# Mixer output of a two-block transformer: gate, grouped norm and output projection in one stage, by token halves

## The chip, the cores and the metric

The kernel runs on one core of a Trainium2 chip. The metric is the time of one execution in microseconds (us), the median of the timed runs. The core has a matrix engine (TensorE, PE in the rows; its weight loads are PEld), a vector engine (VectorE, DVE), an activation engine (ScalarE, ACT), a general engine (GpSimd, POOL) and a sync engine (SyncE, SP) that here only issues transfers. Each engine runs its own instruction list in order; they meet at semaphores.

## The reference

The whole model is two blocks, a mixer with a mixture of experts and then attention with a feed-forward network, for 1024 tokens of width 1024. The change touches the end of the first block's mixer only. There, `y` is the output of the state-space scan (768 channels in 4 groups), `xh` its input, `z` the gate, `y_pool` the 256 channels of a second mixer, `g1` a vector from the conditioning:

```
y = ssd_scan(xh, dt, a, bm, cm) + xh * d_skip
y = y.reshape(b, s, 768) * silu(z)
y = rms_norm(y.reshape(b, s, G, 768 // G)).reshape(b, s, 768)
y_ssd = y * norm_w
mix = concatenate([y_pool, y_ssd], axis=-1) @ w_out
x = x + g1[:, None, :] * mix
h = modulate(x, sh2, sc2)      # its router logits are h @ [w_group, w_router]
```

## The kernel before

Everything is kept transposed: the 128 partitions hold channels, and the free axis the 1024 tokens, so a tensor of 768 channels is 6 tiles of 128x1024 (`SSD_T` = 6) and one of 1024 channels 8 (`KT` = 8). Work is written as stages, one after another. A stage opens its own buffers and semaphores and gives each engine a list; the next stage begins on an engine when all engines have left the one before. Inside a stage `st.dve(ins, "name")` counts an instruction up on its engine's semaphore, and `st.wait(e, st.dve, "name")` waits for it. `settle()` waits for the engine's own last instruction.

`gate_norm` (L963) is the stage after the scan. VectorE makes the gated `y` in place in `xbc[:, 6+j]` with two instructions a tile (L1021, L1023); ScalarE squares it into `zs`, which lies in the buffer of `x` (L1001). TensorE sums the squares over the channels of each group: `member` is a 128x4 matrix of zeros and ones for each tile, so a product with it gives 4 rows of 1024 sums, accumulated over the 6 tiles (L986). VectorE and ScalarE turn these 4x1024 numbers into reciprocal root mean squares (L1025, L1027, L1003). TensorE spreads the 4 rows back over 128 partitions, one product with `member_t` a tile, alternating between two PSUM buffers (L993). Then for each tile VectorE multiplies `y`, the spread factor and the norm weight into `tmp` (L1032), ScalarE rounds it to the high part `xh_mix` (L1006) and GpSimd subtracts to get the low part `xl_mix` (L1013); `tmp` has two buffers, so VectorE waits for GpSimd two tiles back.

`mixer_out` (L1037) is the next stage: 8 output tiles of the projection. Every product of the big projections is made of three, high times high, low times high and high times low (`Gemm.mult`, L239 in the rows): 8 input tiles x 3 x 2 token halves of 512 = 48 matmuls an output tile. The weights of an output tile are 128x1024; they are loaded (L215 for the first two, L200 for the rest), and split into high and low parts by VectorE for the first two (`Gemm.first`, L221 and L223) and by GpSimd for the rest (`Gemm.split`, L207 and L209). VectorE then clears `acc`, scales the router's weights `w_route`, builds `wide` (a matrix of shifts for the router), and for each output tile adds the product to `x` (L1108) and the squares to `acc` (L1111). ScalarE loads `x` back from memory (L1086, 4 MB), as its buffer held `zs`, and later squares and stores `x`.

The next stages (`route`, `experts`) read `x`, `acc` and the logits; they issue their first transfers when `mixer_out` is left.

## Time and profile before

| | |
|---|---|
| median of 3 runs | 2595.18 us (2594.09 to 2597.12) |
| the profiled execution | 2599.4 us, of which the span of the profile is 2597.6 us |
| mean granted TensorE clock | 0.902 of 2.4 GHz |
| TensorE busy (matmul) | 2251.2 us, 87% |
| VectorE busy | 1306.2 us, 50% |
| ScalarE busy | 801.6 us, 31% |
| GpSimd busy | 607.2 us, 23% |

The profile is one execution; times in its rows count from the start of the span. A busy share is a mean over the whole program, and says little on one stage: the stages here take from about 505 to 674 us.

### The profile page before, as it was taken

To read this page: it belongs to the slowest core of one execution; us is meant where nothing else is said; L and a number is where in the kernel's file an instruction comes from. 1 tells how busy PE (TensorE), PEld (TensorE's weight loads), DVE (VectorE), ACT (ScalarE), POOL (GpSimd) and SP (SyncE) were. 2 spreads that over 40 slices of the span, in tenths; PEclk is the share of its full clock that TensorE was granted. 3 is DMA by queue.
4 is the path that set the end of the run, shared out by engine and by line. 5 is a ranking of instruction groups with operands and counts; after the bars stand their busy time and mean duration, and the time that the engine had idled before them with its cause. 6 is when DMAs were issued, how large, how long until landed. Compare 5 with 4: busy or idle time off the path is not lost. (4 is left out here: it accounts for less than half of the span.)

```text
span 2597.6 us, 44356 instructions
## 1 busy us (share of the span) xinstructions
PE 2251.2 (87%) x15928; PEld 1689.1 (65%) x15928; DVE 1306.2 (50%) x1615; ACT 801.6 (31%) x1108; POOL 607.2 (23%) x444
## 2 busy tenths in 40 slices
PE   2699978869754897898977897998999999999998
PEld 1588867638622454454536786776888888888887
DVE  7676165732443686786865536773433213321344
ACT  3211122310233676786863103551210000000013
POOL 0133313222000000000003462222333333333344
PEclk6799977769766998998986998999999999999999
DMA  6333210022699998899954120001111111111113
GB/s 250 144 121 121 91 66 0 1 105 75 254 380 410 363 356 293 320 352 339 337 194 171 57 90 5 0 0 57 48 49 48 49 49 48 48 49 49 48 50 120
DMA packets 103785, 364.19 MB, mean 140 GB/s; under 512 B 7968, under 2 KB 18848, under 8 KB 103344
## 3 DMA queue, kind: packets, MB, share of 16 engines
q1 hardware_dynamic: 85248, 320.43, 34.1%
q10 hardware_dynamic: 13008, 23.07, 2.3%
q0 software_dynamic: 5472, 19.93, 2.2%
q8 instruction: 36, 0.59, 0.1%
q14 instruction: 21, 0.17, 0.0%
HBM read 331.94 MB, written 31.46 MB: 140 GB/s over the span
## 5 line engine op out<-in xcount | busy, mean ns | idle before, releaser
L1488 PE MATMUL moe_hu<-x_res,moe_xt 128*32 128x256 f32 x5120 | 336.4, 406 | 83.2 <-DVE moe_xt L1404 55.7
L1382 DVE COPY x_res<-moew_raw 128x2048 f32 x243 | 270.2, 1135 | 188.0 <-DMA moew_raw<-in_w 110.4
L1488 PEld LDWEIGHTS moe_hu<-x_res,moe_xt 128*32 128x32 f32 x5120 | 163.2, 116 | 213.0 <-issue 90.4
L239 PE MATMUL ff_acc<-ff_yh,ff_w_hi 128*128 128x512 f32 x704 | 274.4, 390 | 0.0
L239 PE MATMUL ff_acc<-ff_yl,ff_w_hi 128*128 128x512 f32 x704 | 273.9, 389 | 0.0
L239 PE MATMUL ff_acc<-ff_yh,ff_w_lo 128*128 128x512 f32 x704 | 273.9, 389 | 0.0
L1382 ACT ACTIVATE x_res<-moew_raw 128x2048 f32 (+1 forms) x121 | 197.2, 1630 | 108.9 <-DMA moew_raw<-in_w 77.7
L207 POOL CAST ff_w_hi<-ff_w_raw 128x1024 fp32r<-128x1024 f32 (+1 forms) x82 | 81.9, 998 | 545.5 <-PE ff_acc L239 545.5
L239 PE MATMUL ff_acc<-xh,ff_w_hi 128*128 128x512 f32 x480 | 188.2, 392 | 7.8 <-DVE ff_w_lo L223 7.1
L239 PE MATMUL in_acc<-xh_mix,in_w_hi 128*128 128x512 f32 x368 | 144.4, 392 | 55.5 <-DVE in_w_lo L223 55.5
L209 POOL TENSOR_TENSOR ff_w_lo<-ff_w_raw,ff_w_hi 128x1024 fp32r<-128x1024 f32 (+1 forms) x82 | 188.7, 2301 | 6.6
L239 PE MATMUL ff_acc<-xh,ff_w_lo 128*128 128x512 f32 x480 | 187.3, 390 | 0.0
L239 PE MATMUL ff_acc<-xl,ff_w_hi 128*128 128x512 f32 x480 | 187.2, 390 | 0.0
L1393 ACT ACTIVATE moe_wdown<-moew_raw 128x2048 f32 x80 | 153.2, 1915 | 25.9 <-PE moe_y L1499 22.0
L1499 PE MATMUL moe_y<-moe_wdown,moe_at 128*32 128x256 f32 x2560 | 157.5, 387 | 2.4 <-ACT moe_at L1533 2.4
L239 PEld LDWEIGHTS ff_acc<-ff_yh,ff_w_hi 128*128 128x128 f32 x704 | 132.1, 188 | 28.0 <-DVE ff_yl L2307 0.5
L239 PEld LDWEIGHTS ff_acc<-ff_yh,ff_w_lo 128*128 128x128 f32 x704 | 132.2, 188 | 27.6
L239 PEld LDWEIGHTS ff_acc<-ff_yl,ff_w_hi 128*128 128x128 f32 x704 | 132.2, 188 | 27.5 <-issue 0.2
L1445 POOL COPY moew_idx<-rows 128x1 int32 (+1 forms) x21 | 11.2, 534 | 578.4 <-PE moe_xturn L1471 578.4
L239 PE MATMUL in_acc<-xl_mix,in_w_hi 128*128 128x512 f32 x368 | 144.1, 392 | 0.0
L239 PE MATMUL in_acc<-xh_mix,in_w_lo 128*128 128x512 f32 x368 | 144.1, 392 | 0.0
L2258 ACT ACTIVATE ff_gs<-ff_gs 128x1024 f32<-128x1024 f32 x22 | 23.3, 1061 | 379.7 <-DVE ff_gs L2318 379.7
(354 smaller groups left out, 3942.3 us busy)
## 6 DMA issues: line engine op xcount, KB each, us to landing
moew_raw<-in_w SPq DMA_DIRECT2D x192, 1024.0 KB, 18.9
ff_w_raw<-in_w_up SPq DMA_DIRECT2D x44, 512.0 KB, 3.3
mid_w_raw<-in_w_qkv SPq DMA_DIRECT2D x24, 512.0 KB, 3.3
in_w_raw<-in_w_in SPq DMA_DIRECT2D x23, 512.0 KB, 3.3
x_res<-in_w_ada SPq DMA_DIRECT2D x20, 512.0 KB, 5.2
y_scratch<-acc_sq ACTq DMA_DIRECT2D x80, 128.0 KB
prep_wa<-in_w_ada SPq DMA_DIRECT2D x18, 512.0 KB, 6.1
ff_w_raw<-in_w_down SPq DMA_DIRECT2D x16, 512.0 KB, 3.3
```

Of the source, the lines that this page charges most:

```text
L207: pool.tensor_copy(hi, raw).then_inc(self.s_hi, 1)
L209: pool.tensor_tensor(lo, raw, hi.bitcast(F32), ALU.subtract).then_inc(self.s_split, 1)
L239: m = pe.matmul(o, w[:, b, k * P:(k + 1) * P], x[:, k, h:h + HALF], start=(k == 0 and t == 0), stop=(k == kt - 1 and t == 2))
L1382: m = e.activation(to, src, ACT.Copy) if k == "act" else e.tensor_copy(to, src)
L1393: m = e.activation(to, src, ACT.Copy) if k == "act" else e.tensor_copy(to, src)
L1445: e.tensor_copy(idx[:, :], self.rows[:, g:g + 1] if isinstance(g, int) else self.rows[:, bass.ds(g, 1)]).then_inc(s_idx, 1)
L1488: m = e.matmul(hu[u % 2][rows(j), 0:2 * FW].rearrange("p (a f) -> p a f", a=2), xt[:, t, rows(u)], w[:, :, FW * j:FW * (j + 1)], start=(t ...
L1499: m = e.matmul(yp[u % 2][rows(j), 0:YW], at[:, t % KC, rows(t // KC)], wdown[:, t, YW * j:YW * (j + 1)], start=(t == 0), stop=(t == FF // ...
L2258: st.act(e.activation(gs[:, :], gs[:, :], ACT.Silu), f"silu{n}")
```

## The change

`gate_norm` is gone as a stage; its work stands at the head of `mixer_out`'s lists.

- Group sums: `member` is padded to 32 columns (4 of them used), and each tile's product is four, one for each quarter of the tokens (256), on the column quarters (0, 32q) of the array. The sums stand on 4 x 32 partitions x 256 tokens in place of 4 x 1024, and so do the two VectorE instructions and the root after them.
- Spreading: in 12 steps (token half h, tile j), each of two products of 256 tokens on the row quarters (64h+32q, 0), which write two PSUM banks. The second `total` buffer is the projection's `acc1`.
- Norm, high and low part: 12 steps of 512 tokens; the product is written in place into `y`; VectorE now makes the low part too, one step behind (`low`).
- The first output tile goes by token halves (`first_product`), each input tile waiting for its own low part.
- The weights and `wr` are requested at the stage's start, behind `member` and `member_t` (now 96 KB and 384 KB); semaphores are cleared after that. VectorE splits the first two weight tiles between the reciprocal and the norm steps. ScalarE loads the table of the root ahead of its wait, and requests `x` right behind the root.
- Clearing `acc`, scaling `w_route` and building `wide` move from VectorE to GpSimd, ahead of its splits. `sq` takes two dead tiles of `xbc`.

The diff, with the removed stage left out (it is printed above):

```
                 self.s_spill = ctx.enter_context(nc.semaphore("x_spilled"))
                 self.mixer_out()
             with self.stage("moew") as self.weights:
@@ -960,100 +959,45 @@
...
-            with st.block() as blk:
...
-        self.keep.close()
...
     def mixer_out(self):
 
         x, acc, ins = self.x, self.acc_sq, self.ins
+        xbc, zs, Q = self.xbc, self.zs, T // 4
         R = EG + NE
         with self.stage("mixout") as st:
             g = Gemm(st)
-            sq, wide, wr = st.sb("sq", [P, 2, T]), st.sb("wide", [P, KT, P]), st.sb("wr", [P, KT, R])
+            wide, wr = st.sb("wide", [P, KT, P]), st.sb("wr", [P, KT, R])
+            sq = xbc[:, 0:2, :]
+            member, member_t = st.sb("member", [P, SSD_T, 32]), st.sb("member_t", [P, SSD_T, P])
+            rstd = st.sb("rstd", [P, Q])
             logits, shifted = st.ps("logits", [P, HALF]), st.ps("shifted", [P, HALF])
-            s_x, s_wr = st.sem("x"), st.sem("wr")
+            group_sum = logits[:, 0:Q]
+            total = [a.rearrange("p (b x) -> p b x", b=2)[:, :, 0:Q] for a in (st.ps("total", [P, T])[:, :], g.acc[1][:, :])]
+            s_x, s_wr, s_member = st.sem("x"), st.sem("wr"), st.sem("member")
+            halves = [slice(h * HALF, (h + 1) * HALF) for h in range(2)]
+            steps = [(h, j) for h in range(2) for j in range(SSD_T)]
+            y = lambda h, j: xbc[:, SSD_T + j, halves[h]]
             with st.block() as blk:
                 @blk.sync
                 def _(e):
+                    e.dma_start(member[:, :, :], ins["member"]).then_inc(s_member, 16)
+                    e.dma_start(member_t[:, :, :], ins["member_t"]).then_inc(s_member, 16)
                     g.first(sp=e, srcs=[ins["w_out"][b] for b in range(2)])
                     e.dma_start(wr[:, :, :], ins["w_route"]).then_inc(s_wr, 16)
+                    self.clear_sems(e)
                     with e.Fori(0, KT // 2 - 1) as i:
                         for b in range(2):
                             g.load(e, i, 2, b, ins["w_out"][2 * i + (2 + b)])
...
                 @blk.gpsimd
                 def _(e):
+                    st.pool.start(e)
+                    st.pool(e.memset(acc[:, :], 0.0))
+                    e.wait_ge(s_wr, 16)
+                    scale, shift = self.mod[:, 32:40], self.mod[:, 24:32]
+                    st.pool(e.tensor_tensor(self.w_route[:, :, :], wr[:, :, :], scale.unsqueeze(2).to_broadcast([P, KT, R]), ALU.mult))
+                    for k in range(KT):
+                        st.pool(e.tensor_scalar(wide[:, k, :], self.const("ones"), shift[:, k:k + 1], None, ALU.mult), "wide")
                     g.after_first(e)
                     with e.Fori(0, KT // 2 - 1) as i:
                         for b in range(2):
...
                 def _(e):
                     st.pe.start(e)
                     e.sem_inc(g.s_mult, 2)
+                    e.wait_ge(s_member, 32)
+                    for j in range(SSD_T):
+                        st.wait(e, st.act, f"gate_sq{j}")
+                        for q in range(4):
+                            m = e.matmul(group_sum[32 * q:32 * q + 32, :], member[:, j, :], zs[:, j, q * Q:(q + 1) * Q],
+                                         start=(j == 0), stop=(j == SSD_T - 1), tile_position=(0, 32 * q))
+                    st.pe(m, "group_sum")
+                    st.wait(e, st.act, "rstd")
+                    for n, (h, j) in enumerate(steps):
+                        if n >= 2:
+                            st.wait(e, st.dve, "normed%d%d" % steps[n - 2])
+                        for q in range(2):
+                            rows = slice(64 * h + 32 * q, 64 * h + 32 * q + 32)
+                            m = e.matmul(total[n % 2][:, q, :], member_t[rows, j, :], rstd[rows, :],
+                                         start=True, stop=True, tile_position=(64 * h + 32 * q, 0))
+                        st.pe(m, f"spread{h}{j}")
+
+                    def first_product():
+                        e.wait_ge(g.s_split, 3)
+                        e.wait_ge(g.s_emptied, 1)
+                        for h in range(2):
+                            for k in range(KT):
+                                if k >= POOL_T:
+                                    st.wait(e, st.dve, f"lo{h}{k - POOL_T}")
+                                for t, (w, xs) in enumerate(((g.hi, self.xh), (g.hi, self.xl), (g.lo, self.xh))):
+                                    m = e.matmul(g.acc[0][:, halves[h]], w[:, 0, k * P:(k + 1) * P], xs[:, k, halves[h]],
+                                                 start=(k == 0 and t == 0), stop=(k == KT - 1 and t == 2))
+                        m.then_inc(g.s_mult, 1)
 
...
                     for k in range(KT):
-                        g.mult(e, k // 2, 0, k % 2, self.xh, self.xl)
+                        if k:
+                            g.mult(e, k // 2, 0, k % 2, self.xh, self.xl)
+                        else:
+                            first_product()
                         if k == 0:
-                            st.wait(e, st.dve, "wide")
+                            st.wait(e, st.pool, "wide")
                             for j in range(KT):
                                 m = e.matmul(shifted[:, 0:R], wide[:, j, :], wr[:, j, :], start=(j == 0), stop=(j == KT - 1))
...
                 @blk.scalar
                 def _(e):
                     st.act.start(e)
+                    for j in range(SSD_T):
+                        st.wait(e, st.dve, f"gated{j}")
+                        st.act(e.activation(zs[:, j, :], xbc[:, SSD_T + j, :], ACT.Square), f"gate_sq{j}")
+                    e.preload_act_table(ACT.Sqrt)
+                    st.wait(e, st.dve, "inv")
+                    st.act(e.activation(rstd[:, :], rstd[:, :], ACT.Sqrt), "rstd")
                     e.dma_start(x[:, :, :], self.xt_dram).then_inc(s_x, 16)
+                    for h, j in steps:
+                        st.wait(e, st.dve, f"normed{h}{j}")
+                        st.act(e.activation(self.xh[:, POOL_T + j, halves[h]], y(h, j), ACT.Copy), f"hi{h}{j}")
                     for k in range(KT):
                         g.emptied(e, k // 2, 0, k % 2)
                         if k >= 2:
...
                 def _(e):
                     st.dve.start(e)
                     e.sem_inc(g.s_emptied, 2)
+                    for j in range(SSD_T):
+                        st.dve(e.scalar_tensor_tensor(xbc[:, SSD_T + j, :], xbc[:, j, :], self.col("d_skip", j), xbc[:, SSD_T + j, :], ALU.mult, ALU.add))
+                        st.dve.settle()
+                        st.dve(e.tensor_tensor(xbc[:, SSD_T + j, :], xbc[:, SSD_T + j, :], zs[:, j, :], ALU.mult), f"gated{j}")
+                    st.wait(e, st.pe, "group_sum")
+                    st.dve(e.tensor_scalar(rstd[:, :], group_sum, GROUPS / (SSD_T * P), EPS, ALU.mult, ALU.add))
+                    st.dve.settle()
+                    st.dve(e.reciprocal(rstd[:, :], rstd[:, :]), "inv")
                     g.first(by=e)
-                    st.dve(e.memset(acc[:, :], 0.0))
-                    e.wait_ge(s_wr, 16)
-                    scale, shift = self.mod[:, 32:40], self.mod[:, 24:32]
-                    st.dve(e.tensor_tensor(self.w_route[:, :, :], wr[:, :, :], scale.unsqueeze(2).to_broadcast([P, KT, R]), ALU.mult))
-                    for k in range(KT):
-                        st.dve(e.tensor_scalar(wide[:, k, :], self.const("ones"), shift[:, k:k + 1], None, ALU.mult), "wide")
+
+                    def low(h, j):
+                        st.wait(e, st.act, f"hi{h}{j}")
+                        st.dve(e.tensor_tensor(self.xl[:, POOL_T + j, halves[h]], y(h, j), self.xh[:, POOL_T + j, halves[h]].bitcast(F32), ALU.subtract), f"lo{h}{j}")
+                    for n, (h, j) in enumerate(steps):
+                        st.wait(e, st.pe, f"spread{h}{j}")
+                        yq = y(h, j).rearrange("p (b x) -> p b x", b=2)
+                        st.dve(e.scalar_tensor_tensor(yq, yq, self.col("ssd_norm_w", j), total[n % 2], ALU.mult, ALU.mult), f"normed{h}{j}")
+                        if n:
+                            low(*steps[n - 1])
+                    low(*steps[-1])
+                    st.wait(e, st.pool, "wide")
                     e.wait_ge(s_x, 16)
                     for k in range(KT):
                         g.ready(e, k // 2, 0, k % 2)
...
+        self.keep.close()
...
-    member = (group.T[:, :, None] == np.arange(GROUPS)).astype(f)
+    member = (group.T[:, :, None] == np.arange(32)).astype(f)
...
-        "member_t": np.ascontiguousarray(member.transpose(2, 1, 0)),
+        "member_t": np.tile(np.ascontiguousarray(member.transpose(2, 1, 0)), (4, 1, 1)),
```

## Rows read from the trace of the kernel before

**Rows 1.** Windows: us, busy of PE, PEld, DVE, ACT, POOL; PE clock, DMA share, GB/s.

```profile
505.00:520.00 15.00, 10.60 (x19) 1.84 (x20) 14.38 (x13) 5.29 (x5) 0.00 (x0) 0.77 0.01 2
...
535.00:558.00 23.00, 18.19 (x22) 6.64 (x20) 7.68 (x6) 6.34 (x6) 14.06 (x6) 0.50 0.00 0
558.00:567.50 9.50, 0.00 (x0) 0.00 (x0) 1.89 (x2) 0.00 (x0) 0.01 (x1) 0.50 0.92 378
567.50:573.00 5.50, 5.42 (x13) 4.25 (x14) 0.03 (x1) 0.00 (x0) 0.00 (x0) 0.51 0.90 375
...
583.00:674.00 91.00, 90.79 (x464) 77.21 (x463) 25.26 (x17) 8.16 (x8) 19.14 (x11) 1.00 0.19 70
```

**Rows 2.** Timeline, all engines, group sums to first norm step: start us, us.

```profile
520.38 1.06 ACT L1001 ACTIVATE x_res<-xbc 128x1024 f32<-128x1024 f32 x1 [1.40 <-DVE xbc L1023]
...
521.49 1.88 PE L986 MATMUL gate_group_sum<-x_res,gate_member 128*4 128x512 f32 x4 [0.57 <-ACT x_res L1001]
...
523.41 1.21 DVE L1025 TENSOR_SCALAR gate_rstd<-gate_group_sum 4x1024 f32<-4x1024 f32 x1 [3.06 <-PE gate_group_sum L986]
524.66 6.54 DVE L1027 RECIPROCAL gate_rstd<-gate_rstd 4x1024 f32<-4x1024 f32 x1
531.23 1.05 ACT L1003 ACTIVATE gate_rstd<-gate_rstd 4x1024 f32<-4x1024 f32 x1 [8.49 <-DVE gate_rstd L1027]
...
532.34 20.84 PE L993 MATMUL gate_total<-gate_rstd,gate_member_t 4*128 4x512 f32 x24 [8.97 <-ACT gate_rstd L1003]
...
536.16 1.28 DVE L1032 SCALAR_TENSOR_TENSOR gate_tmp<-xbc,cols,gate_total 128x1024 f32<-128x1024 f32 x1 [4.96 <-PE gate_total L993]
```

**Rows 3.** Timeline, from the last low part to the projection's first matmul.

```profile
555.67 2.34 POOL L1013 TENSOR_TENSOR xl_mix<-gate_tmp,xh_mix 128x1024 fp32r<-128x1024 f32 x1 [1.07 <-ACT xh_mix L1006]
558.31 0.81 SPq L215 DMA_DIRECT2D mixout_w_raw<-in_w_out  x2
558.40 0.38 ACTq L1086 DMA_DIRECT2D x_res<-xt_scratch  x1
...
565.58 0.69 DVE L221 CAST mixout_w_hi<-mixout_w_raw 128x1024 fp32r<-128x1024 f32 x1 [11.07 <-DMA mixout_w_raw<-in_w_out]
566.30 1.23 DVE L223 TENSOR_TENSOR mixout_w_lo<-mixout_w_raw,mixout_w_hi 128x1024 fp32r<-128x1024 f32 x1
...
567.58 0.79 PE L239 MATMUL mixout_acc<-xh_mix,mixout_w_hi 128*128 128x512 f32 x1 [14.39 <-DVE mixout_w_lo L223]
```

**Rows 4.** Groups by form, TensorE: busy us, mean ns of one, idle before.

```profile
L1488 PE MATMUL moe_hu<-x_res,moe_xt 128*32 128x256 f32 x5120 | 336.4, 406 | 83.2 <-DVE moe_xt L1404 55.7 <-ACT x_res L1382 16.2 <-DVE x_res L1382 9.8
...
L2006 PE MATMUL att_scores<-att_dist,att_qs 64*128 64x256 f32 x224 | 56.0, 390 | 0.0
...
L993 PE MATMUL gate_total<-gate_rstd,gate_member_t 4*128 4x512 f32 x24 | 20.8, 1063 | 9.0 <-ACT gate_rstd L1003 9.0
```

**Rows 5.** Groups by form on VectorE, ScalarE and GpSimd, for shapes that are new here.

```profile
L1588 DVE COPY acc_sq<-moe_y 128x256 f32<-128x256 f32 x80 | 33.3, 416 | 4.1 <-PE moe_y L1499 4.1
...
L1848 DVE TENSOR_TENSOR qkv<-mid_acc,mid_rows 128x512 f32<-128x512 f32 x12 | 8.3, 692 | 48.7 <-PE mid_acc L239 48.7
...
L2101 DVE RECIPROCAL att_rden<-att_sums 128x4 f32<-128x4 f32 x32 | 5.7, 178 | 1.1
...
L727 DVE SCALAR_TENSOR_TENSOR xl_mix<-in_mix,cols,xh_mix 128x512 fp32r<-128x512 f32 x4 | 2.9, 748 | 3.3 <-ACT xh_mix L646 3.2
...
L895 ACT ACTIVATE ssd_btok<-ssd_states 128x512 f32<-128x512 f32 x8 | 4.8, 597 | 35.5 <-PE ssd_states L835 35.5
...
L1967 POOL COPY acc_sq<-qkv 128x128 f32<-128x128 f32 x2 | 0.6, 288 | 0.0
```

**Rows 6.** Timeline of GpSimd and VectorE in the projection's last rounds.

```profile
646.11 2.41 POOL L209 TENSOR_TENSOR mixout_w_lo<-mixout_w_raw,mixout_w_hi 128x1024 fp32r<-128x1024 f32 x1
...
647.31 2.30 DVE L1111 TENSOR_TENSOR acc_sq<-acc_sq,mixout_sq 128x1024 f32<-128x1024 f32 x1 [1.13 <-ACT mixout_sq L1091]
...
660.03 1.23 DVE L1111 TENSOR_TENSOR acc_sq<-acc_sq,mixout_sq 128x1024 f32<-128x1024 f32 x1 [1.12 <-ACT mixout_sq L1091]
```

More of the change, by code:

```diff
@@ L996, in _ @@
-                @blk.scalar
-                def _(e):
-                    st.act.start(e)
-                    for j in range(SSD_T):
-                        st.wait(e, st.dve, f"gated{j}")
-                        st.act(e.activation(zs[:, j, :], xbc[:, SSD_T + j, :], ACT.Square), f"sq{j}")
-                    st.wait(e, st.dve, "inv")
-                    st.act(e.activation(rstd[:, :], rstd[:, :], ACT.Sqrt), "rstd")
-                    for j in range(SSD_T):
-                        st.wait(e, st.dve, f"normed{j}")
-                        st.act(e.activation(self.xh[:, POOL_T + j, :], tmp[:, j % 2, :], ACT.Copy), f"hi{j}")
@@ L1034, in gate_norm @@
-        self.keep.close()
-    def mixer_out(self):
-        x, acc, ins = self.x, self.acc_sq, self.ins
-        R = EG + NE
-        with self.stage("mixout") as st:
-            g = Gemm(st)
-            sq, wide, wr = st.sb("sq", [P, 2, T]), st.sb("wide", [P, KT, P]), st.sb("wr", [P, KT, R])
-            logits, shifted = st.ps("logits", [P, HALF]), st.ps("shifted", [P, HALF])
-            s_x, s_wr = st.sem("x"), st.sem("wr")
-            with st.block() as blk:
-                @blk.sync
-                def _(e):
+                    e.dma_start(member[:, :, :], ins["member"]).then_inc(s_member, 16)
```

60 lines of the change are left out of this document (6 added, 54 removed).

## The prediction

> **What bounds the kernel now.** I read the page's busy shares first (TensorE 87%), then the windows of the stretch that the change touches, then its timeline, and last the groups by form for durations. The busy share misleads here: the reader is to see in the windows that from 505 to 520 us VectorE is busy 14.38 of 15 us, from 535 to 558 no engine but TensorE is near full, and that one at a granted clock of 0.50 (1.2 of 2.4 GHz), and from 558 to 567.5 nothing computes but 1.89 us on VectorE, while the transfers run at 92% [rows 1]. So three limits follow one another: VectorE's gating, a chain of single instructions, and a wait for weights.
>
> The timeline gives the chain [rows 2, 3]. The last square ends at 521.44. TensorE's last sums are read at 523.41 (1.97 later). VectorE takes 1.21 for scale and EPS and 6.54 for the reciprocal, to 531.20. The root (1.05) and the first tile's spreading bring VectorE's first norm step to 536.16 (4.96 later). The last low part ends at 555.67 + 2.34 = 558.01, 21.85 after the first norm step began. The weights are requested only then (558.31), VectorE starts on them 7.27 later, and TensorE's first projection matmul is at 567.58 (9.57 after the last low part). From 521.44 to 567.58 that is 46.14 us. From 567.58 on TensorE is the bound; the change leaves its matmuls there as they are.
>
> **The change, part by part,** from the end of the last square.
>
> *Group sums on column quarters.* A tile's last group is now 8 records (two for each fp32 matmul) of 256 columns. Are the quarters concurrent? The experts' matmuls of form 128*32 with 256 columns stand on four column quarters: 5120 records cover 336.4 us, 66 ns each, while the 64*128 form with the same 256 columns covers 56.0 us with 224, 250 ns each [rows 4]. So column quarters overlap nearly fourfold. Four records of 512 columns took 1.88 us at the full clock [rows 2]; two rounds of 256 take half of that or less, twice that at the half clock. I take 1.1 us to VectorE's read, for 1.97: 0.9 gained.
>
> *Reciprocal root on 128 x 256.* The scale from PSUM takes 0.42 for 256 columns [rows 5] in place of 1.21. The reciprocal goes by columns, 0.178 for 4 [rows 5] and 6.54 for 1024 [rows 2], so 0.178 + 252 x 6.24 ns = 1.75. Gained 0.8 + 4.8.
>
> *Weights' split between reciprocal and norm.* VectorE does 2 x (0.69 + 1.23) plus gaps = 3.95 us [rows 3] ahead of the first norm step. Beside it ScalarE's root (about a quarter of 1.05 and a fixed part, 0.4) and the first spread (1.3 to 2.1) end earlier, so the split hides them: 3.95 in place of 4.96, 1.0 gained. What stands behind this wait on VectorE is all of the norm. Its two weight tiles were 7.3 us under way before, beside the 4 MB of `x` [rows 3]; now they are asked for at the stage's start, some 20 us before use, behind 0.5 MB of constants. `x` itself is requested some 18 us ahead of the first product, for 9.2 before. TensorE's new wait for the constants has slack too: the sums of a tile take 1 us and VectorE's gating makes one in 2.4, so they may land as late as the fourth tile. VectorE's wait for `wide` comes after the last low part, when GpSimd has long been done. The second pair of loads, which waits on SyncE for the split, starts then too, far ahead of GpSimd's use of it.
>
> *The steps.* VectorE does 12 times a norm of 512 (0.748, the nearest row with PSUM input and a per-partition factor) and a low part of 512 (0.69) [rows 5]; with two gaps of 0.03 that is 1.50 us a step. ScalarE's high part is 0.60 [rows 5], shorter than the norm step that covers it. GpSimd's 2.34 per tile [rows 3] is off the path. The spread of a step is four records of 256 columns. A record of 512 columns at the half clock takes 20.84 / 24 = 0.87 [rows 4], so one of 256 takes 0.43. If the two row quarters overlap, a step's spread takes 0.85; if not, 1.71. No row shows row quarters beside one another; the nearest that shows parts of the array overlap is the column form, so I take the overlap. Then VectorE bounds: the norm of step 9 ends 0.78 + 8 x 1.50 + 0.75 = 13.5 after the first began, spread 11 follows (0.05 + 0.85), and the first product stands right behind it in TensorE's list: 14.45 us in place of 21.85, and its first half needs only low parts that are long done. The second half needs the last low part some 2 us after the product began, and 24 matmuls of the first half come before.
>
> The Trainium skill (TensorE: Matmul & The Clock Gate, Part 3, "What overlaps and what doesn't") says that matmuls in different row groups start about 4 ns apart. By that page the overlap holds and the sum stays; without it the sum would be 3.4 us less, as worked out below from rows. No row here shows it.
>
> *No second stage, no wait for weights.* The 9.57 us from the last low part to the first matmul go.
>
> *Moved to GpSimd.* In time it is hidden: `wide` is needed after the first product, some 40 us later. But it lies beside VectorE's gating, which is the bound from 505 to 520. The nearest rows: the adding of squares takes 2.30 beside GpSimd's subtraction and 1.23 without it, with an overlap of 648.52 - 647.31 = 1.21; so VectorE loses 0.88 of each microsecond of overlap [rows 6]. GpSimd's work is eight of 128x128 (0.288 each by the copy of that shape, 2.3 in all [rows 5]), one of 288 columns (2.41 x 288/1024 = 0.7 [rows 6]), and a clearing that reads nothing (at most the 1.0 or so that its row share would give). Bounds: nothing lost, and 4.0 x 0.88 = 3.5. I take the reading ones, 3.0 us at 0.8: 2.4 us lost, on the path.
>
> The Trainium skill (GPSIMD Engine Reference, 1. Specifications) lists the two engines' SBUF interface as shared, with contention when VectorE has two SBUF inputs, as all of the gating has. By that rule the loss is near its upper bound and the sum 1.1 us less. The trace agrees for the subtraction, in the 2.30 and 1.23 above.
>
> *Sum.* Before 46.14. After: 2.4 + 1.1 + 0.46 + 1.75 + 3.95 + 14.45 = 24.1. Gain 22.0 us. All behind it, the routing's and experts' transfers included, is issued relative to the end of the stage, so it moves as a block. The profiled execution was 2599.4 (span 2597.6), 4.2 above the median; it would become 2577.4, and the median 2595.18 - 22.0 = 2573.2 us.
>
> **The rivals.**
>
> *Row quarters one after another.* The change does not do what it says in its second half. Spread n waits for norm n-2, and TensorE bounds: the first product starts 0.78 + 10 x 1.71 = 17.9 us after the first norm step, 3.4 later. For it: the 250 ns a record of the 64*128 form [rows 4], no less than one record alone. Against: those stand on one row half at a time. 2576.6 us.
>
> *The clock is up when the first product starts.* At present the projection's first 5.3 us go at the half clock: window clock 0.51, then 1.00 [rows 1]. If the new spreading, with 32 rows a tile in place of 4, raises it, the 12 slow matmuls save about 0.2 us each: 2.5 us, 2570.7. Against: TensorE was busy 18.19 of 23 us in the spreading and the clock stayed at 0.50 [rows 1].
>
> *The contention is at its upper bound, or GpSimd's scaled copies are twice as long as the copy row.* 1 to 3 us: 2574 to 2576.
>
> *Slower: the clock stays at half in the projection.* Place: the 91 us from 583 to 674, now at 1.00 [rows 1]. Each microsecond of work done at half clock costs another, so the gain of 22 is eaten once 22 us of full-clock work runs at half, that is a stretch of 44 us at 0.50; from 27 us of such work on the kernel is slower by over 0.2%, at 35 it is 2595 + 13 = 2608 us. Against: after 44 us at half clock before 573 the dense product raised it within 5.5 us [rows 1], and the same product now follows.
>
> *Late weights.* The split stands ahead of all norms in VectorE's list; each microsecond that the weights land after about 527 costs one. Against: 7.3 us under way before. It would need 22 us of delay for no gain.
>
> **How the numbers follow.** Main case 0.56 (2573.2), row quarters in turn 0.17 (2576.6), clock up early 0.10 (2570.7), more contention 0.10 (2575), slower 0.02, and 0.05 for an unforeseen wait of more than 5 us, late weights among them, that leaves the kernel between 2580 and 2593. The range: below, no contention (2.4) and the early clock (2.5) with it give 2568.3; above, row quarters in turn with full contention (1.1 + 3.4) give 2577.7, and some microseconds for a wait that I don't see. 2567 to 2581. A measurement of this kernel tells about 0.2% (5.2 us) from no change. Faster by more 0.96, within it 0.02, slower by more 0.02.
>
> **What would show it.** Right: a reciprocal of 1.75 us; norm and low of 0.75 and 0.69 in a rhythm of 1.5 us; TensorE's first projection matmul at about 567.58 - 22.0 = 545.6 us of the span; no idle VectorE between the reciprocal and the split; VectorE's gating some 2.4 us longer. A rhythm of 1.71 with VectorE waiting for TensorE shows the first rival. Wrong: VectorE waiting for the weights' transfer, GpSimd's `wide` still running when the gating ends, or a projection whose windows stay at 0.50.

## The result and the profile after

The changed kernel takes 2564.98 us (median of 4 runs, 2562.76 to 2568.68), beside 2594.64 for the kernel before in the same comparison (4 runs, 2593.3 to 2597.12): 29.7 us less, a ratio of 0.9886 with an interval of 0.9869 to 0.9903. The forecast was 22.0 us less, 2573.2 in a range of 2567 to 2581. So the direction was right and the gain a third larger than forecast; the time lies 2 us below the range. The profiled execution took 2562.76 us (span 2560.9).

In the profiles I compare two pieces of the span throughout. The *stretch* runs from VectorE's first gating instruction to TensorE's first projection matmul; the *projection* from there to VectorE's copy of the routing logits. In the two first profiles the stretch is 62.05 us before and 36.43 after (505.53 to 567.58, and 501.14 to 537.57), so 25.6 less where 22.0 were forecast; the projection is 106.31 and 105.59.

The windows of the changed kernel's stretch answer to [rows 1] (us, busy time and records of PE, PEld, DVE, ACT, POOL; granted clock, DMA share, GB/s):

```profile
501.00:517.00 16.00, 5.41 (x40) 1.01 (x40) 15.29 (x12) 5.61 (x6) 9.17 (x7) 0.59 0.31 105
517.00:524.70 7.70, 3.16 (x16) 1.37 (x16) 5.67 (x6) 2.43 (x3) 1.85 (x4) 0.50 0.39 136
524.70:537.50 12.80, 11.71 (x40) 5.14 (x40) 12.76 (x21) 6.30 (x10) 0.00 (x0) 0.50 0.77 328
...
537.50:541.50 4.00, 4.00 (x12) 3.12 (x11) 2.68 (x5) 1.26 (x2) 0.00 (x0) 0.52 0.02 4
541.50:545.00 3.50, 3.50 (x17) 2.88 (x16) 0.00 (x0) 0.00 (x0) 0.00 (x0) 1.00 0.00 0
```

The reader is to see one engine in all three windows of the stretch. VectorE is busy 15.29 of 16.0, 5.67 of 7.7 and 12.76 of 12.8 us: the window in which nothing computed but 1.89 us on VectorE is gone, and the transfers (the 16 DMA engines are busy 77% of that window) lie beneath the norm. The clock is up 3.8 us after the first product began, for 5.3 before.

The timeline has the chain, line for line against [rows 2, 3]:

```profile
508.51 1.28 DVE L1083 SCALAR_TENSOR_TENSOR xbc<-xbc,cols 128x1024 f32<-128x1024 f32 x1
508.71 1.61 POOL L998 TENSOR_TENSOR w_route<-mixout_wr,mod 128x288 f32<-128x288 f32 x1 [6.76 <-DMA mixout_wr<-in_w_route]
509.82 1.57 DVE L1085 TENSOR_TENSOR xbc<-xbc,x_res 128x1024 f32<-128x1024 f32 x1
510.38 8.48 POOL L1000 TENSOR_SCALAR mixout_wide<-consts,mod 128x128 f32<-128x128 f32 x8
...
516.67 1.06 ACT L1063 ACTIVATE x_res<-xbc 128x1024 f32<-128x1024 f32 x1 [1.56 <-DVE xbc L1085]
...
517.78 1.08 PE L1014 MATMUL mixout_logits<-x_res,mixout_member 128*32 128x256 f32 x8 [1.54 <-ACT x_res L1063]
518.93 0.42 DVE L1087 TENSOR_SCALAR mixout_rstd<-mixout_logits 128x256 f32<-128x256 f32 x1 [2.29 <-PE mixout_logits L1014]
519.39 1.75 DVE L1089 RECIPROCAL mixout_rstd<-mixout_rstd 128x256 f32<-128x256 f32 x1
521.06 0.63 DVE L221 CAST mixout_w_hi<-mixout_w_raw 128x1024 fp32r<-128x1024 f32 x1
...
521.64 1.22 PE L1023 MATMUL mixout_total<-mixout_rstd,mixout_member_t 32*128 32x256 f32 x4 [2.78 <-ACT mixout_rstd L1066]
...
523.58 1.22 DVE L223 TENSOR_TENSOR mixout_w_lo<-mixout_w_raw,mixout_w_hi 128x1024 fp32r<-128x1024 f32 x1
524.73 0.74 DVE L1098 SCALAR_TENSOR_TENSOR xbc<-xbc,cols,mixout_total 128x512 f32<-128x512 f32 x1
...
529.32 0.74 DVE L1098 SCALAR_TENSOR_TENSOR xbc<-xbc,cols,mixout_total 128x512 f32<-128x512 f32 x1
529.98 0.69 DVE L1094 TENSOR_TENSOR xl_mix<-xbc,xh_mix 128x512 fp32r<-128x512 f32 x1
...
530.58 0.74 DVE L1098 SCALAR_TENSOR_TENSOR xbc<-xbc,cols,mixout_acc 128x512 f32<-128x512 f32 x1
...
537.57 0.80 PE L1035 MATMUL mixout_acc<-xh_mix,mixout_w_hi 128*128 128x512 f32 x1
```

From the last square's end (517.73) to the first product are 19.84 us, for 46.14 before. The reciprocal has no idle time behind it, and neither has the split. A norm step and a low part repeat every 1.26 us (529.32, 530.58), not every 1.50. A step's spread (1.22 us for its four records, at a granted clock of 0.50) is shorter than that, so VectorE bounds the steps, and the row quarters do run beside one another. The eight scaled copies end at 518.86, 2.2 us after VectorE's gating; nothing on the path waits for them.

### The profile page after: what moved, and what is told of

The parts are those of the page before. It is cut to its first block and busy times, and to the rows that moved or that the text cites. A ratio compares the mean times of both kernels' runs of the same rounds, so it can differ in the third digit from the quotient of the medians.

```text
span 2560.9 us, 44454 instructions
## 1 busy us (share of the span) xinstructions
PE 2234.8 (87%) x15976; PEld 1684.7 (66%) x15976; DVE 1305.0 (51%) x1623; ACT 803.1 (31%) x1114; POOL 604.5 (24%) x448
## 5 line engine op out<-in xcount | busy, mean ns | idle before, releaser
L239 PEld LDWEIGHTS ff_acc<-ff_yh,ff_w_hi 128*128 128x128 f32 x704 | 132.1, 188 | 28.4 <-DVE ff_yl L2305 0.5
```

The costliest lines, as they stand in the source:

```text
L239: m = pe.matmul(o, w[:, b, k * P:(k + 1) * P], x[:, k, h:h + HALF], start=(k == 0 and t == 0), stop=(k == kt - 1 and t == 2))
```

## The experiments

All numbers in one table: stretch and projection from the one profile of each kernel, the timed median (its range), and the ratio to the kernel before in the same comparison, with its interval. The medians of the kernel before in the four comparisons were 2597.03, 2594.62, 2595.73 and 2594.03 us.

| run | stretch | projection | median (range) | ratio |
|---|---|---|---|---|
| b_again | 61.27 | 106.62 | 2596.59 (2589.84–2598.31) | 0.9993 [0.9981, 1.0005] |
| a_again | 36.56 | 105.17 | 2567.88 (2565.09–2568.60) | 0.9891 [0.9874, 0.9907] |
| e_two_stages | 45.12 | 106.08 | 2578.13 (2577.44–2580.47) | 0.9932 [0.9916, 0.9949] |
| e_no_half | 39.39 | 105.66 | 2570.10 (2569.25–2573.27) | 0.9901 [0.9884, 0.9918] |
| e_prelude_dve | 35.74 | 105.80 | 2567.95 (2562.90–2574.21) | 0.9904 [0.9878, 0.9930] |
| e_pool_later | 36.44 | 105.60 | 2569.21 (2565.07–2570.59) | 0.9898 [0.9873, 0.9923] |
| e_second_split_later | 34.28 | 106.26 | 2566.89 (2566.55–2569.62) | 0.9891 [0.9868, 0.9914] |
| e_full_rows | 36.67 | 103.87 | 2568.39 (2566.62–2571.66) | 0.9902 [0.9877, 0.9926] |
| b_third | 62.27 | 106.37 | 2595.56 (2589.50–2604.67) | 1.0001 [0.9990, 1.0012] |
| a_third | 36.55 | 105.59 | 2567.38 (2567.22–2572.67) | 0.9896 [0.9881, 0.9912] |
| e_best_quarters | 33.99 | 106.37 | 2567.30 (2563.18–2573.59) | 0.9884 [0.9866, 0.9902] |
| e_best_rows | 35.29 | 103.91 | 2565.69 (2565.06–2566.36) | 0.9884 [0.9867, 0.9901] |
| e_after_delay1 | 36.54 | 105.15 | 2566.70 (2562.52–2567.22) | 0.9892 [0.9875, 0.9909] |
| e_before_delay3 | 62.11 | 106.08 | 2596.90 (2590.92–2599.84) | 1.0008 [0.9998, 1.0019] |
| b_fourth | 62.08 | 106.17 | 2599.47 (one run) | |
| a_fourth | 36.58 | 105.52 | 2565.37 (one run) | |

An interval is some 3 to 7 us wide on either side, so an edit worth 1 or 2 us is judged by stretch and projection in the profiles. Over four profiles the stretch repeats within 0.15 us in the changed kernel and 1.0 in the kernel before, the projection within 0.45 in both. Each edited kernel has one profile.

### Both kernels again (b_again, a_again)

No edit.

> The kernel before again, for a second profile of it. Theory A: its stretch is 62.1 us again, and its parts outside the stretch differ from its own first profile by as much as the changed kernel's do (4 us ahead of the stretch, 6 behind). Theory B: its parts outside the stretch repeat within 1 us, longer than the changed kernel's.

> The changed kernel again. Theory A (the gain is made between the end of the scan and the projection's first matmul, the rest of the difference of the two profiles is variation between executions): from the first gating instruction to the first projection matmul 36.4 us again (62.1 before), and the parts ahead of and behind that stretch differ from the first profile by some us in either direction; median gain over before 25 to 27 us. Theory B (the change also shortens something outside the stretch, in the scan or the experts): that stretch 36.4 us, but the parts outside are again 4 us and more shorter than before's, and the median gain is 29 to 31 us.

The ratio of the change holds. The stretch is 24.7 us shorter in this pair, and the stretch alone is not the whole gain: the medians differ by 29.15 us, where the first theory had 25 to 27.

### The gate's part alone (e_two_stages)

The kernel before, with the new gate arithmetic (column quarters, reciprocal root on 128 x 256, half steps with VectorE's low parts), but two stages as before, with the weights asked for and split behind the gate stage. From its diff against the kernel before:

```diff
-            rstd, tmp = st.sb("rstd", [GROUPS, T]), st.sb("tmp", [P, 2, T])
+            rstd = st.sb("rstd", [P, Q])
...
+                                m = e.matmul(group_sum[32 * q:32 * q + 32, :], member[:, j, :], zs[:, j, q * Q:(q + 1) * Q],
+                                             start=(j == 0), stop=(j == SSD_T - 1), tile_position=(0, 32 * q))
...
+                            low(*steps[n - 1])
```

> The new gate and norm (sums and spreading on quarters, low part on VectorE) as a stage of its own, then the projection's stage as before. What is taken out of the change: early weights and their split, the first product by halves, GpSimd's part. Theory A: the projection's first matmul comes 9.6 us after the last low part as before, the split of 3.7 us is no longer ahead of the norm steps (the first spread bounds there, about 2 us), so the stretch is 36.4 - 0.7 (contention) - 1.6 + 2.7 + 9.6 = 46.4 us and the gain 15.7 us. Theory B: 4 us more than that if what helps outside comes with the gate's arithmetic, 15.7 if it comes with the merge.

The stretch is 45.12 us. So the arithmetic is worth 16.8 (mean stretch of the four profiles before, 61.92, less 45.12), and all the rest of the change 8.6 more (45.12 less 36.5): one stage with early weights, the first product by halves, and GpSimd's part, which costs. The expectation had 46.4, as it took 9.6 us from the last low part to the first product. Timed, the two stages are 10 us slower than the changed kernel in the same comparison (2578.13 and 2567.88). The timeline shows where the second part lies:

```profile
541.38 1.48 DVE L1029 TENSOR_TENSOR xl_mix<-xbc,xh_mix 128x512 fp32r<-128x512 f32 x2
...
543.13 0.81 SPq L215 DMA_DIRECT2D mixout_w_raw<-in_w_out  x2
...
549.27 0.69 DVE L221 CAST mixout_w_hi<-mixout_w_raw 128x1024 fp32r<-128x1024 f32 x1 [6.42 <-DMA mixout_w_raw<-in_w_out]
550.00 1.23 DVE L223 TENSOR_TENSOR mixout_w_lo<-mixout_w_raw,mixout_w_hi 128x1024 fp32r<-128x1024 f32 x1
551.28 0.80 PE L239 MATMUL mixout_acc<-xh_mix,mixout_w_hi 128*128 128x512 f32 x1 [11.06 <-DVE mixout_w_lo L223]
```

The wait of VectorE for weights is back (6.42 us), with 8.4 us, not 9.6, from the last low part (542.86) to the first product.

### The first product waits for all low parts (e_no_half)

```diff
+                        st.wait(e, st.dve, f"lo1{SSD_T - 1}")
```

> As the change, but the first product waits for the last low part of the second token half. Theory A: the first matmul comes right after the last low part, 540.3 in place of 537.6 on the changed kernel's profile, 2.7 us later, so the halves are worth 2.7 us: gain 2.7 us less than the change's. Rival: the first product then waits for nothing else and TensorE's clock, idle a little longer, is no different, so the same 2.7; if the clock rises later by one step the loss is up to 4 us.

Stretch 39.39, 2.8 us more than the unedited one beside it (36.56). Here TensorE starts after the last low part's end (541.47 + 1.48 = 542.95) at 543.10. The overlap by halves is worth 2.8 us; the projection stays at 105.66, so it is not given back there.

### The routing prelude on VectorE (e_prelude_dve)

The clearing, the 288 scaled columns and the eight scaled copies move from GpSimd to VectorE, behind its last low part.

```diff
-                    st.pool(e.memset(acc[:, :], 0.0))
...
-                        st.pool(e.tensor_scalar(wide[:, k, :], self.const("ones"), shift[:, k:k + 1], None, ALU.mult), "wide")
...
+                    st.dve(e.memset(acc[:, :], 0.0))
...
+                        st.dve(e.tensor_scalar(wide[:, k, :], self.const("ones"), shift[:, k:k + 1], None, ALU.mult), "wide")
```

> As the change, but the clearing of acc, the scaled router weights and wide are made by VectorE right behind the last low part, where it waits for the first product anyway; GpSimd has only its splits. Theory A (GpSimd's work beside the gating costs the path 0.7 us, not the 2.4 forecast): gating goes back to 14.8 us from 15.5, the stretch from the first gating instruction to the first projection matmul is 35.7 us for 36.4, the rest is the same. Rival (the move was free or a gain): 36.4 us or more.

This measures the contention. From the first gating instruction to the reciprocal are 17.56 us, for 18.25 to 18.40 in the changed kernel's four profiles: GpSimd beside the gating cost 0.8 us, not 2.4. VectorE does the prelude beneath TensorE's products:

```profile
543.24 0.40 DVE L1099 TENSOR_TENSOR w_route<-mixout_wr,mod 128x288 f32<-128x288 f32 x1
543.55 1.65 DVE L1101 TENSOR_SCALAR mixout_wide<-consts,mod 128x128 f32<-128x128 f32 x8
```

1.65 us for eight of them, for 8.48 on GpSimd in the changed kernel. Of those, the five that ran beside the gating took 1.31 to 1.50 us each, and the three behind it 0.60.

### GpSimd's prelude behind the reciprocal (e_pool_later)

```diff
+                    st.wait(e, st.dve, "inv")
```

> As the change, but GpSimd starts its clearing, router weights and wide only after the reciprocal. Theory A: gating 14.8 us, and now the weights' split and the first low parts of VectorE (two SBUF inputs) lie beside it; they lose about as much as the gating did, so the stretch stays at 36.4 within 0.5 us. Rival: VectorE loses 0.88 of each microsecond there as the adding of squares did, 6 us of GpSimd work cost up to 5 us.

The gating is again 17.58 us to the reciprocal (0.8 less), but from the reciprocal to the product it takes 18.87 for 18.18: the contention only moved. The timeline shows it in the split of weights:

```profile
523.55 1.22 DVE L223 TENSOR_TENSOR mixout_w_lo<-mixout_w_raw,mixout_w_hi 128x1024 fp32r<-128x1024 f32 x1
524.37 0.93 POOL L999 TENSOR_TENSOR w_route<-mixout_wr,mod 128x288 f32<-128x288 f32 x1
524.70 1.16 DVE L221 CAST mixout_w_hi<-mixout_w_raw 128x1024 fp32r<-128x1024 f32 x1
525.37 4.89 POOL L1001 TENSOR_SCALAR mixout_wide<-consts,mod 128x128 f32<-128x128 f32 x6
525.89 1.27 DVE L223 TENSOR_TENSOR mixout_w_lo<-mixout_w_raw,mixout_w_hi 128x1024 fp32r<-128x1024 f32 x1
```

The second cast, an instruction with one input, took 1.16 us while GpSimd's part was under way; in the changed kernel it took 0.69.

### The second weight tile split behind the low parts (e_second_split_later)

As e_pool_later, and VectorE splits tile 0 ahead of the norm and tile 1 behind the last low part.

```diff
-                    g.first(by=e)
+                    g.first(by=e, bs=(0,))
...
+                    g.first(by=e, bs=(1,))
```

> As the one before (GpSimd after the reciprocal), and the second weight tile is split after the last low part in place of before the norm steps. Theory A: a cast and a subtraction (0.69 + 1.23, less 0.1 of overlap) leave the path, and the first spread ends just when VectorE comes: the stretch is 34.6 us, 1.8 less. The second tile is needed 13 us after the first product began and is split 2 us after the last low part, so nothing waits for it. Rival: TensorE's spreading bounds the first step and only 1 us comes off.

The stretch is 34.28, 2.2 us less than e_pool_later's. The tile's split is 1.8 of it, as forecast (1.86 us from the split's start to the first norm, for 3.67 in the changed kernel); the rest is mainly the slow cast, which is gone. The split of two tiles is on the path, as the forecast had it; the root and the first spread would let VectorE begin the norm after one:

```profile
525.16 1.23 DVE L223 TENSOR_TENSOR mixout_w_lo<-mixout_w_raw,mixout_w_hi 128x1024 fp32r<-128x1024 f32 x1
526.35 0.75 DVE L1099 SCALAR_TENSOR_TENSOR xbc<-xbc,cols,mixout_total 128x512 f32<-128x512 f32 x1
```

But 0.7 us is given back: the projection is 106.26 for 105.60. The product starts earlier and the clock does not rise earlier with it. The windows of this kernel, whose first product begins at 539.53, have the half clock for 5.3 us, where e_pool_later had it for 3.8:

```profile
539.50:544.80 5.30, 5.30 (x15) 4.13 (x13) 4.47 (x7) 1.26 (x2) 0.00 (x0) 0.50 0.01 3
544.80:548.00 3.20, 3.20 (x15) 2.63 (x14) 0.00 (x0) 0.00 (x0) 0.00 (x0) 1.00 0.51 164
```

### Spreading over all 128 rows (e_full_rows)

The membership matrix is masked for each quarter, so that every spread contracts over all rows and lands the same sums; no two can run beside one another.

```diff
-                            m = e.matmul(total[n % 2][:, q, :], member_t[rows, j, :], rstd[rows, :],
-                                         start=True, stop=True, tile_position=(64 * h + 32 * q, 0))
+                            m = e.matmul(total[n % 2][:, q, :], member_t[:, 2 * h + q, j, :], rstd[:, :],
+                                         start=True, stop=True)
```

> As the change, but each spreading product runs on all 128 rows of the array, with a member matrix that is zero outside its quarter, so two products of a step can't run beside one another. Theory A (row quarters ran side by side, 0.9 us a step): a step's spreading takes 4 x 0.43 = 1.7 us at the half clock and bounds the step for 1.26, the first projection matmul comes 4.5 to 5 us later: stretch 41.2 us. Rival (the activity on all rows raises the clock): the steps go back to 1.26 us after some microseconds, the stretch is 38 us or less and the first product's slow matmuls are gone, 2.4 us off the projection. If row quarters had not run side by side, the stretch would stay 36.4.

The edit also makes the constants of the spreading four times as large (1.5 MB for 384 KB). TensorE's first group sums come 6.7 us after the gating began, for 4.6, and still end in time; GpSimd's work starts later too, and the gating takes 16.54 us to the last square's end, for 16.59 to 16.74.

The timeline shows both what the overlap is worth in itself and why it is worth nothing here:

```profile
526.02 2.07 PE L1022 MATMUL mixout_total<-mixout_rstd,mixout_member_t 128*128 128x256 f32 x4 [2.78 <-ACT mixout_rstd L1065]
...
529.90 1.91 PE L1022 MATMUL mixout_total<-mixout_rstd,mixout_member_t 128*128 128x256 f32 x4
...
531.64 1.03 PE L1022 MATMUL mixout_acc<-mixout_rstd,mixout_member_t 128*128 128x256 f32 x4
...
533.90 1.13 PE L1022 MATMUL mixout_acc<-mixout_rstd,mixout_member_t 128*128 128x256 f32 x4
```

At the half clock a step takes 2.07 us for 1.22 on quarters. But the clock does not stay there. The windows of this kernel:

```profile
529.00:531.50 2.50, 2.40 (x6) 1.41 (x6) 2.23 (x4) 1.26 (x2) 0.00 (x0) 0.50 0.98 423
531.50:542.00 10.50, 9.60 (x36) 5.91 (x35) 10.16 (x17) 4.96 (x8) 0.00 (x0) 1.00 0.71 299
542.00:547.00 5.00, 5.00 (x24) 4.16 (x23) 3.23 (x6) 1.34 (x3) 0.00 (x0) 1.00 0.01 3
```

It is at 2.4 GHz from 531.5 on, 5.5 us after the first spread began, where with quarters it stayed at 1.2 GHz through 12 us of spreading. The steps then take 1.13, below VectorE's 1.26, and the projection begins at the full clock: 103.87 us for 105.59. The stretch is 0.2 longer; together 1.5 us less than the changed kernel. So the rival of the expectation came in, not its first theory (a stretch of 41.2). The edit changes two things at once, how many rows of the array a spread runs on and how long TensorE is busy with a step; which of them raises the clock is not separated.

### Two further versions (e_best_quarters, e_best_rows), beside both kernels (b_third, a_third)

e_best_quarters joins e_prelude_dve's edit and the later second split (not GpSimd's wait). e_best_rows is that, with full rows.

> The kernel before a third time. Theory A: its scan can come out anywhere between 134.5 and 137.6 us, as it did in the seven profiles of kernels with the merged stage, and its experts between 636 and 643. Theory B: scan 137.4 us again, for the fourth time in kernels with a stage of its own for the gate.

> The changed kernel a third time, on one chip with a third run of the kernel before. Theory A: stretch 36.4 us and projection 105.4 (before: 61.3 to 62.1 and 106.4), all else alike within the spread between executions: the scan 134.5 to 137.6 us for either kernel, the experts 636 to 643 for either. Median gain 26 us. Theory B (something outside is shortened for good): the scan near 134.7 in the changed kernel and 137.4 in the one before once more, and a gain of 29 us.

> As the change, with two moves: the second weight tile is split after the last low part, and the clearing of acc, the router weights and wide are made by VectorE behind that, GpSimd has only its splits. From the profiles of the two moves alone: gating 0.7 us shorter, the split before the norm steps 1.8 us for 3.7, and no contention behind the reciprocal: stretch 33.6 us (36.4 for the change), projection as before, 105.4. Gain over the kernel before by the stretch and the projection 29.0 us, 2.8 more than the change's 26.2. If VectorE's 5 us of moved work reach the first product's end, the projection gets longer.

> As e_best_quarters, and the spreading on all 128 rows of the array (zeros outside the quarter). Theory: the first spread takes 2.1 us at the half clock for 1.2, now uncovered by the shorter split, so the stretch is 34.6 to 35 us; the clock is up when the first product starts, so the projection is 104 us for 105.4. Sum of both 138.6 to 139, within 0.5 us of e_best_quarters: rows and quarters are worth the same. Rival: the quarters are the better choice by the 5 us that their concurrency was priced at (3.4 in the prediction).

The kernels of before and after repeat: stretch 62.27 and 36.55, medians 28.35 us apart, where the first theory had 26. Their scans took 135.94 and 134.25 us.

e_best_quarters misses its forecast: the stretch is 33.99 (33.6 expected) and the projection 106.37 (105.4), as the clock rises 5.5 us after the first product began, again later than in the changed kernel. e_best_rows has 35.29 (34.6 to 35) and 103.91 (104). Its spreading raises the clock again, 3.7 us after it began:

```profile
522.80:526.50 3.70, 3.66 (x9) 2.95 (x10) 2.05 (x3) 0.63 (x1) 0.00 (x0) 0.50 0.90 310
526.50:538.30 11.80, 10.77 (x41) 6.63 (x40) 11.66 (x19) 5.67 (x9) 0.00 (x0) 1.00 0.71 303
```

By stretch and projection they come to 140.4 and 139.2 us, for 142.0 in the mean of the changed kernel's four profiles (36.53 and 105.47). Timed, both stand at 0.9884, the changed kernel at 0.9896 beside them, and the intervals overlap: the 1.6 and 2.8 us are seen in one profile each and not settled by the times. Nor are the 1.2 us between rows and quarters, which the expectation had within 0.5.

### A later start (e_after_delay1, e_before_delay3), beside both kernels (b_fourth, a_fourth)

Outside the stretch, the scan ahead of it differed (from VectorE's first instruction that writes `ssd_xdt` to its first gating instruction): it took 134.25 to 135.09 us in the changed kernel's first three profiles and 135.94 to 137.44 in the kernel before's. To see if the point at which the clock falls in the scan depends on when it starts, GpSimd's first work there is put behind one or three extra copies.

```diff
+                    for n in range(3):
+                        e.tensor_copy(xdte[:, :].rearrange("p (j t) -> p j t", t=CH), xbc[:, 0:SSD_T, cols(0)]).then_inc(s_delay, 1)
+                        e.wait_ge(s_delay, n + 1)
```

> The changed kernel with one extra copy of 128x768 (0.9 us, its result unused) on GpSimd ahead of the scan's first step, nothing else. In the three profiles of the changed kernel the scan took 134.3 to 135.1 us, and the clock's falls in it came 0.9 us later against the scan's start than in the others, 135.9 to 137.6. Theory C (the scan's time hangs on where its steps meet the rises and falls of the granted clock, and not on the merge): 0.9 us later start brings the falls to where they are in the kernel before, the scan takes about 137.5 us, 3 us longer for 0.9 us of delay. Rival (the merge itself shortens the scan): 134.7 us plus nothing.

> The kernel before with three such copies (2.7 us) ahead of the scan. Theory C: the scan from its first step on takes 134.5 to 135.5 us where the delay puts the falls as in the changed kernel, so 2.7 us of added work cost nothing or nearly; a start at another place gives up to 137.5. Rival: scan 137.4 us and the whole 2.7 us slower.

> A fourth profile of the kernel before. If the place belongs to the program: a scan of 135.9 to 137.5 us again, falls at 26.3 to 27.3 us. If it is chance: 134.3 is as likely.

> A fourth profile of the changed kernel. If the place at which the scan meets the clock's falls belongs to the program: falls 27.9, 45.0 and 62.1 us after the scan's start and a scan of 134.2 to 135.1 us again. If it is chance: anywhere to 137.6.

The scan took 137.58 us with one copy, as the theory had it, and 136.22 with three in the kernel before, where it had 134.5 to 135.5. But a_fourth, with no copy, also took 137.31 (b_fourth 137.50), so the delay is not shown to be the cause. Two other kernels with the one merged stage and an unedited scan, e_full_rows and e_best_quarters, took 137.58. So a shorter scan is not a fixed property of the changed program. The scan's windows, of the changed kernel's first profile and then of a_fourth, have the same work (778 records of TensorE, mean clock 0.69) in another time:

```profile
366.60:501.10 134.50, 114.29 (x778) 105.43 (x776) 82.62 (x88) 36.44 (x48) 46.06 (x31) 0.69 0.08 32
```

```profile
368.10:505.40 137.30, 115.08 (x778) 104.73 (x776) 82.59 (x88) 36.12 (x48) 46.07 (x31) 0.69 0.08 31
```

This fits clock levels that meet other work from one execution to the next. What sets them was not found.

## Which steps of the prediction held, and which failed

The chain of waits came out as forecast, and the gain did not: 29.7 us for 22.0. Three terms failed. "3.0 us at 0.8: 2.4 us lost" for GpSimd's work beside the gating measured 0.7. The rhythm of "1.50 us a step", 14.45 us to the first product, measured 1.26 and 12.84. And "it moves as a block" put at nothing whatever lies outside the stretch, where the profiles show 0.9 us in the projection, 0.9 in the routing, and more whose cause stays open. Counted as in the forecast's sum, on the first profile of each kernel:

| term | forecast | measured |
|---|---|---|
| GpSimd beside the gating | 2.4 | 0.7 |
| sums, to VectorE's read | 1.1 | 1.20 |
| scale | 0.46 | 0.46 |
| reciprocal | 1.75 | 1.67 |
| split of weights | 3.95 | 3.67 |
| steps to the first product | 14.45 | 12.84 |
| sum, for 46.14 before | 24.1 | 20.5 |

**The contention, "2.4 us lost, on the path": mis-sized by 1.7.** From the first gating instruction to the last square's end are 16.59 us, for 15.91 before, and e_prelude_dve confirms 0.8. I had carried over the 0.88 us lost for each microsecond of overlap from [rows 6], where GpSimd subtracts with two inputs. GpSimd's scaled copies have one, and there it was mostly GpSimd that gave way: 1.31 to 1.50 us for each of the five beside the gating, for 0.60 behind it, while VectorE's instructions beside them took 0.05 to 0.11 longer, 0.3 in all. About as much, 0.35, was lost in one place, by the instruction that began at 509.82 while GpSimd scaled the router's weights, with two inputs; the one that had begun at 508.51, ahead of that, kept its 1.28. Whether the number of inputs decides or which instruction began first, no run separates. So the price was too high, and the durations too short: the copies and the scaling took 10.1 us of GpSimd, not 3.0. One sign that the prediction had named for being wrong did appear, `wide` still running when the gating ends; it cost nothing, as the first to wait for it is VectorE behind its last low part (540.27). Of the bounds, the lower, nothing lost, was the nearer. The Trainium skill (GPSIMD Engine Reference, 1. Specifications) states that the two contend when VectorE has two SBUF inputs; the 0.8 us agrees in kind and shows how little it can be.

**The rhythm, "1.50 us a step": mis-sized by 0.24.** Over eight steps that is 1.9 us; the last spread takes back 0.3 (1.21 us from the end of step 9's norm to the first product, for 0.9), which leaves 1.6. The durations were right; the groups by form of the changed kernel answer to [rows 5]:

```profile
L1094 DVE TENSOR_TENSOR xl_mix<-xbc,xh_mix 128x512 fp32r<-128x512 f32 x12 | 8.2, 686 | 0.1
...
L1098 DVE SCALAR_TENSOR_TENSOR xbc<-xbc,cols,mixout_total 128x512 f32<-128x512 f32 x6 | 4.5, 744 | 0.0
```

What was wrong is "with two gaps of 0.03". 744 and 686 ns make 1.43, and the rhythm is 1.26: the next instruction's record begins about 0.08 us before the last one's ends. The trace of before had this already, in VectorE's gating:

```profile
506.85 1.23 DVE L1023 TENSOR_TENSOR xbc<-xbc,x_res 128x1024 f32<-128x1024 f32 x1
507.99 1.28 DVE L1021 SCALAR_TENSOR_TENSOR xbc<-xbc,cols 128x1024 f32<-128x1024 f32 x1
```

506.85 + 1.23 is 508.08, and the next starts at 507.99. I had taken the gaps from places where the next instruction needs the last one's result (524.66 after 523.41 + 1.21 in [rows 2]). The split (0.28) and the reciprocal (0.08) are off for the same reason.

**The steps' bound: right, with less to spare.** Row quarters overlap (1.22 us a step, not 1.71), so the first rival did not come in; but a step's spread lasts 1.22, not the 0.85 of the forecast, which costs 0.3 once, behind the last norm that the first product waits for. The Trainium skill (TensorE: Matmul & The Clock Gate, Part 3, "The mechanism") has it that matmuls in different row groups of the array overlap, and 1.22 beside the 2.07 of full rows agrees. What neither the forecast nor the rival had is that TensorE's clock would rise with spreads on all 128 rows, which is why a spread of 2.07 us at the half clock costs nothing net. (Where the prediction says that "the sum" would be 3.4 or 1.1 us less, it is the gain that would be less.)

**The clock at the projection: partly the rival's.** I kept 5.3 us at the half clock; it was 3.8. Over the four profiles each the projection is 0.9 us shorter (106.37 and 105.47). With the clock up from the start, e_full_rows has 103.87, which is 2.5 less than 106.37 and the rival's full price.

**Late weights, a clock that stays low: neither.** VectorE did not wait for the split's tiles, and the clock was at 1.00 from 541.5 on.

**Outside the stretch: assumed to move as a block.** Over four profiles of each kernel, stretch and projection account for 26.3 us of the gain (25.4 and 0.9), and the times give 28.4 to 29.7. The routing (from the copy of the logits to the experts' first matmul, `moe_hu`) is 0.9 shorter (means 55.37 and 54.49; single profiles of both kernels reach 54.78). The rest lies in the scan (means 137.1 and 135.3) and the experts (from there to the first matmul into `mid_turned`: 641.5 and 638.2), which vary by 3 and by 4 to 6 us between profiles of one kernel. Part of that is the draw of the profiles, which differ by 32.1 us in the mean, more than the times. Over all eleven profiles with the merged stage (without e_after_delay1) the means are 136.1 and 639.7, over the five with two stages (without e_before_delay3) 137.15 and 641.1: 1.1 and 1.4 us apart. Whether the change has a hand in it stays open: single profiles can't tell, and the delays didn't.

**The range.** Its lower end took in no contention and an early clock, 2568.3, and I treated the durations and gaps as exact. With the measured 20.5 for 24.1 the sum gives 2569.6, inside the range; with the projection's and the routing's 0.9 each, 2567.8. The last 2.8 us down to 2564.98 are the part that stays open. The two repeats of the changed kernel came to 2567.88 and 2567.38, just inside the range, so the 2 us beyond its edge are no more than the spread of a median; the 6 to 8 us beyond the forecast gain are not.

## What to carry to other kernels

A sum of many short instructions of one engine goes by the distance between two starts in the trace, not by durations and a gap; here that was 16% of a step. A price of contention belongs to one pair of operations: the row from which it is taken should match in the inputs of both sides and in which of the two begins first, as these runs don't tell the two apart. An edit that starts the next work earlier can lose a part of it again to the clock, as the later split did (2.2 us off the stretch, 0.7 onto the projection). Before packing small matmuls onto parts of the array, look at the granted clock: if TensorE isn't the bound in that stretch, the same matmuls over all rows can bring it up for what follows, as they did in both kernels that had them.

## What was not expected of the hardware

- With full-row spreads the clock rose to 2.4 GHz 5.5 us after they began in one kernel and 3.7 in the other; with quarter-row spreads of the same columns, TensorE busy 11.71 of 12.8 us, it stayed at 1.2 GHz. The projection behind full rows took 103.87 and 103.91 us, for 105.2 to 105.6 in the changed kernel.
- A scaled copy of 128x128 took 0.60 us on GpSimd alone and 1.31 to 1.50 beside VectorE's gating, which lost 0.05 to 0.11 us an instruction by it. Eight took 1.65 us on VectorE.
- One program's scan took 134.25 to 137.31 us in four profiles, at the same mean clock of 0.69.
